# A three-layer transformer block on one core: weight splits of the first stage on VectorE, the norm sum in two products, products of constants at stage ends, and a sparse stage in another order

## The reference

```python
for i in range(DEPTH):                       # layer a, then layer b
    hn = rms_norm(x, norm_gain[i])
    y = mixer_a(hn, ...) if i % 2 == 0 else mixer_b(hn, ...)
    x = x + y
h = rms_norm_2(x, norm_g) * (1.0 + scale) + shift
p = h @ w_in                                 # r, k, v, decay, q, latent, index, gates
y_a = rwkv7_branch(...)
# sparse: index scores, the 128 best keys of each query, softmax over those
score = einsum('bqh,bqhs->bqs', wi_b, relu(einsum('bqhd,bsd->bqhs', qi_b, ki)))
_, sel = lax.top_k(score, topk)
p = softmax(logits + bias); y_b = einsum('bqhk,bqkc->bqhc', p, lat_sel) @ w_uv
x = x + gate * ((sigmoid(g_a) * br_a + sigmoid(g_b) * br_b) @ w_o)
```

## Time and profile before

| | |
|---|---|
| median of 3 runs | 1619.67 us (1618.01 to 1620.99) |
| the profiled execution | 1620.39 us, its span 1618.6 us |
| busy: PE, PEld, DVE, ACT, POOL | 94%, 75%, 50%, 48%, 48% of the span |
| mean granted TensorE clock | 0.981 of full |
| stage_in | 0 to 25.6 us |
| layer a | 26.5 to 661.4 us |
| layer b | 662.4 to 980.2 us |
| modulated projections, sparse attention | 981.2 to 1186.6 us |
| recurrent branch and the rest | from 1187.4 us |

### The profile page before, as it was taken

How to read it: one execution, slowest core, us unless ns; L and a number is a source line. 1 busy time by engine, 2 the same in 40 slices (tenths; PEclk the granted TensorE clock), 3 DMA queues, 4 the chain that set the end, 5 groups by cost and what they waited for, 6 DMA issues and landing times. The chain is left out here.

```text
span 1618.6 us, 29747 instructions
## 1 busy us (share of the span) xinstructions
PE 1520.7 (94%) x11588; PEld 1218.7 (75%) x11588; DVE 804.2 (50%) x1936; ACT 772.5 (48%) x1557; POOL 782.5 (48%) x477
## 2 busy tenths in 40 slices
PE   5999999999999999899999998998968998899997
PEld 4888787878888788667777775676757886678876
DVE  4145455454545456344454323398247753354545
ACT  4654637364553643366665633346654432442322
POOL 4734436262534543466545443236657651475551
PEclk8999999999999999899999999999979999999999
DMA  6333132231413221454444115232010001333331
GB/s 140 110 88 108 53 95 85 76 108 53 121 40 108 64 84 53 89 161 145 137 139 123 53 53 157 52 73 59 8 29 3 4 17 28 79 105 97 97 93 53
DMA packets 239124, 130.98 MB, mean 81 GB/s; under 512 B 28646, under 2 KB 233518, under 8 KB 238968
## 3 DMA queue, kind: packets, MB, share of 16 engines
q1 hardware_dynamic: 231448, 114.09, 25.5%
q10 hardware_dynamic: 7536, 14.98, 3.2%
HBM read 126.62 MB, written 2.43 MB: 80 GB/s over the span
## 5 line engine op out<-in xcount | busy, mean ns | idle before, releaser
L1596 POOL TENSOR_TENSOR w_low<-a_w_raw,w_high 128x1024 fp32r<-128x1024 f32 x70 | 173.2, 2476 | 56.3 <-ACT w_high L1483 56.3
L314 PE MATMUL a_proj<-h_low,w_high 128*128 128x512 f32 x488 | 195.9, 402 | 1.2 <-POOL h_low L1614 1.2
L316 PE MATMUL a_proj<-h_high,w_high 128*128 128x512 f32 x488 | 192.1, 394 | 0.0
L315 PE MATMUL a_proj<-h_high,w_low 128*128 128x512 f32 x488 | 191.3, 392 | 0.0
L1609 POOL TENSOR_TENSOR a_sq_low<-a_sq,a_sq_high 128x512 fp32r<-128x512 f32 x48 | 62.9, 1310 | 249.8 <-ACT a_sq_high L1507 249.8
L895 POOL TENSOR_TENSOR w_low<-b_w_raw,w_high 128x1024 fp32r<-128x1024 f32 x40 | 100.4, 2511 | 97.2 <-ACT w_high L729 97.2
L314 PE MATMUL b_proj<-h_low,w_high 128*128 128x512 f32 x288 | 116.4, 404 | 1.4 <-POOL h_low L934 0.8
L316 PE MATMUL b_proj<-h_high,w_high 128*128 128x512 f32 x288 | 113.1, 393 | 0.0
L315 PE MATMUL b_proj<-h_high,w_low 128*128 128x512 f32 x288 | 113.1, 393 | 0.0
L314 PEld LDWEIGHTS a_proj<-h_low,w_high 128*128 128x128 f32 x488 | 91.7, 188 | 24.0 <-issue 1.4
L316 PEld LDWEIGHTS a_proj<-h_high,w_high 128*128 128x128 f32 x488 | 91.7, 188 | 20.3
(11 more groups left out here) (534 smaller groups left out, 4148.1 us busy)
## 6 DMA issues: line engine op xcount, KB each, us to landing
a_w_raw<-in_a_w_in_dram SPq DMA_DIRECT2D x78, 512.0 KB, 3.8
b_w_raw<-in_b_w_in_dram SPq DMA_DIRECT2D x30, 512.0 KB, 4.1
b_ada_w<-in_ada_w_dram ACTq DMA_DIRECT2D x24, 512.0 KB, 3.7
f_wt<-in_w_in_dram SPq DMA_DIRECT2D x19, 512.0 KB, 3.8
sparse_w_raw<-in_w_in_dram SPq DMA_DIRECT2D x17, 512.0 KB, 3.9
a_bias<-scr_a SPq DMA_DIRECT2D x32, 128.0 KB
a_w_raw<-in_a_w_out_dram SPq DMA_DIRECT2D x8, 512.0 KB, 4.3
b_w_raw<-in_b_w_out_dram SPq DMA_DIRECT2D x8, 512.0 KB, 4.2
```

The costliest lines, as they stand in the source:

```text
L314: nc.tensor.matmul(out, lh, rl, start=first, stop=False)
L315: nc.tensor.matmul(out, ll, rh, start=False, stop=False)
L316: return nc.tensor.matmul(out, lh, rh, start=False, stop=last)
L1596: nc.gpsimd.tensor_tensor(low(slot_of(b)), raw[:, n % RAW, :, :], high(slot_of(b)), ALU.subtract).then_inc(s_wl, 1)
```

## The change

Four groups of edits:

1. stage_in: ACT rounds block 0 only, after its last table copy; DVE rounds block 1 and makes both `w_low`; POOL makes none.
2. Norm sum of layers a and b: the eighth square is no longer added by DVE. TensorE multiplies the sum of seven by ones, then the eighth square by ones, into the same bank.
3. `idle_products`: products of a constant 128 x 128 tile with itself, whose result nobody reads: 24 after the last table copy of bank 0 in stage_in, 20 after each norm sum, 10 ahead of the first product of `first_two` (layers a, b and the modulated projections).
4. sparse_attention: the projection work is spread over one more slot (34, so part 1 of the last step has work too); ACT copies both turned tiles before the exponentials; the tanh moves to step 0; the rounds of the search go from four a step in steps 0 to 7 to four in steps 0 to 3 and two or three in steps 4 to 10; POOL mixes unit 4 before it splits; the last unit's parts are added by DVE.

```diff
 stage_in
-                for j in range(PRE):
-                    pool.wait_ge(s_wh, j + 1)
-                    nc.gpsimd.tensor_tensor(T.wl[:, j, :, :], raw[:, j, :, :], T.wh[:, j, :, :], ALU.subtract).then_inc(s_wl, 1)
...
+                pe.wait_ge(s_ones_r, 1)
+                pe.wait_ge(s_rows, 4)
+                idle_products(nc, T, ps_rows[:, 0, 0:P], 24)
...
+                dve.wait_ge(s_w[1], 16)
+                nc.vector.tensor_copy(T.wh[:, 1, :, :], raw[:, 1, :, :]).then_inc(s_wh[1], 1)
+                for j in (1, 0):
+                    dve.wait_ge(s_wh[j], 1)
+                    nc.vector.tensor_tensor(T.wl[:, j, :, :], raw[:, j, :, :], T.wh[:, j, :, :], ALU.subtract).then_inc(s_wl, 1)
...
+def idle_products(nc, T, out, count):
+    for _ in range(count):
+        nc.tensor.matmul(out, T.pair_ones_r, T.pair_ones_r, start=True, stop=True)
...
 def first_two
+    idle_products(nc, T, outs[0][:, 0:P], 10)
...
 layers a and b, TensorE and VectorE
-            pe.wait_ge(s_acc, KT - 1)
-            nc.tensor.matmul(ps_ss[:, :], T.ones, T.rn[:, :], start=True, stop=True).then_inc(s_nss, 1)
+            pe.wait_ge(s_acc, KT - 2)
+            nc.tensor.matmul(ps_ss[:, :], T.ones, T.rn[:, :], start=True, stop=False)
+            pe.wait_ge(s_nsq, KT)
+            nc.tensor.matmul(ps_ss[:, :], T.ones, sq[:, (KT - 1) % 2, :], start=False, stop=True).then_inc(s_nss, 1)
+            idle_products(nc, T, ps_proj[:, 0, :][:, 0:P], 20)
...
-                if m >= 2:
+                if 2 <= m < KT - 1:
                     add_square(nc, dve, T, sq, s_nsq, s_acc, m - 1)
-            add_square(nc, dve, T, sq, s_nsq, s_acc, KT - 1)
+                if m == KT - 2:
+                    add_square(nc, dve, T, sq, s_nsq, s_acc, m)
...
 sparse_attention
-        rest, slots = NU * KT - sum(issue), 2 * STEPS + 1
+        rest, slots = NU * KT - sum(issue), 2 * STEPS + 2
...
-                for h in range(2):
-                    if t:
-                        keep_pt(t - 1, h)
-                    if t < STEPS:
-                        exps(t, h)
+                if t:
+                    keep_pt(t - 1, 0)
+                    keep_pt(t - 1, 1)
                 if t < STEPS:
                     for h in range(2):
+                        exps(t, h)
+                    for h in range(2):
                         divide(t, h)
...
+            search = {t: (2, 2) for t in range(HP)}
+            search.update({t: (1, 2 if t % 5 == 4 else 1) for t in range(HP, 3 * HP - 1)})
...
-                if t < 2 * HP:
-                    top_rounds(2)
+                early, late = search.get(t, (0, 0))
+                top_rounds(early)
...
+            u = NU - 1
+            dve.wait_ge(s_pt_k, u + 1)
+            nc.vector.tensor_tensor(T.tile(plan[u][1]), now[:, (u - 4) % 2, :], before[:, (u - 4) % 2, :], ALU.add)
```

More of the change, by code:

```diff
@@ L174, in stage_in @@
         s_w = [sem(f"si_w{j}") for j in range(PRE)]
-        s_wh, s_wl = sem("si_w_high"), sem("si_w_low")
+        s_wh, s_wl = [sem(f"si_w_high{j}") for j in range(PRE)], sem("si_w_low")
         A, B, C, TREL = range(4)
@@ L275, in _ @@
                     nc.scalar.activation(sq[:, k, :], T.X0[:, k, :], ACT.Square).then_inc(s_sq, 1)
-                nc.scalar.activation(T.pair_ones_r, T.pair_ones, ACT.Copy)
+                nc.scalar.activation(T.pair_ones_r, T.pair_ones, ACT.Copy).then_inc(s_ones_r, 1)
                 act.wait_ge(s_rowmm, 1)
@@ L322, in first_block, with first_two @@
     return w_in[:, :, L.w_cols(j, 0):L.w_cols(j, 0) + P]
-def first_two(pe, matmul, outs, high, low, T, s_hh, s_low, done):
+def first_two(pe, nc, outs, high, low, T, s_hh, s_low, done):
+    matmul = nc.tensor.matmul
+    idle_products(nc, T, outs[0][:, 0:P], 10)
     for k in range(KT):
@@ L660, in _ @@
             slots = [slot_of(("ring", u)) for u in range(2)]
-            first_two(pe, nc.tensor.matmul, [proj_bank(u) for u in range(2)], [wh[:, i] for i in slots], [wl[:, i] for i in slots],
+            first_two(pe, nc, [proj_bank(u) for u in range(2)], [wh[:, i] for i in slots], [wl[:, i] for i in slots],
                       T, s_hh, s_low, s_proj)
@@ L1472, in _ @@
             pe.wait_ge(s_ln, NQK * PAIRS)
-            pe.wait_ge(s_acc, KT - 1)
-            nc.tensor.matmul(ps_ss[:, :], T.ones, T.rn[:, :], start=True, stop=True).then_inc(s_nss, 1)
+            pe.wait_ge(s_acc, KT - 2)
+            nc.tensor.matmul(ps_ss[:, :], T.ones, T.rn[:, :], start=True, stop=False)
+            pe.wait_ge(s_nsq, KT)
+            nc.tensor.matmul(ps_ss[:, :], T.ones, sq[:, (KT - 1) % 2, :], start=False, stop=True).then_inc(s_nss, 1)
+            idle_products(nc, T, out_bank(3)[:, 0:P], 20)
         @block.scalar
@@ L1940, in _ @@
         def _(pe):
-            first_two(pe, nc.tensor.matmul, [ps[:, u, :] for u in range(2)], [wh[:, slot(u)] for u in range(2)],
+            first_two(pe, nc, [ps[:, u, :] for u in range(2)], [wh[:, slot(u)] for u in range(2)],
                       [wl[:, slot(u)] for u in range(2)], T, s_hh, s_low, s_proj)
@@ L2216, in _ @@
                     turn(t - 1, 1)
-                if t < STEPS:
-                    steps(part_at(t, 1))
+                steps(part_at(t, 1))
                 if t:
@@ L2315, in after @@
                 for u in done_at[pos]:
-                    if u + RING < NU:
+                    if u != 4 and u + RING < NU:
                         split_low(u + RING)
```

41 lines of the change are left out of this document (21 added, 20 removed).

## The result

| | before | changed |
|---|---|---|
| median | 1621.22 us (20 runs, 1618.01 to 1628.03) | 1612.86 us (20 runs, 1608.92 to 1621.13) |
| ratio, 95% interval | | 0.9948 (0.9939 to 0.9958) |
| the profiled execution, its span | 1620.39 us, 1618.6 us | 1611.21 us, 1609.4 us |
| mean granted clock | 0.981 | 0.987 |

The change makes the kernel 8.4 us faster by the medians and 9.2 us by the two profiled executions. Forecast were 12.9 us, 1607.5 us. The sign held, and so did the range for 8 in 10 (1602 to 1616); the forecast's own range (1604 to 1611) was missed by 1.9 us. The gain is a third less than forecast, and its parts have other sizes than the prediction gave them.

The account below looks back on a forecast made before the run. TensorE was taken as the bound nearly everywhere, with gains only at its waits, lower-clock stretches and stage ends on other engines. 3.2 + 5.5 + 0.9 + 3.3 = 12.9 us gave 1607.5 us; own range 1604 to 1611, 8 in 10 1602 to 1616.

Parts of the forecast that it names:

- Term 1: In stage_in, moved roundings and subtractions let ACT, DVE, TensorE and SP all end at 22.4 us, not 25.58: 3.2 us.
- The price of a narrow product: A 128-column fp32r product on TensorE was taken to cost 0.11 us, the spacing of 256 columns.
- Term 2: Idle products keep TensorE's clock up at the starts of layers a, b and the modulated projections: 5.5 us together.
- I take it that it stays at 1.00: With TensorE's gaps cut to about one us or less, the granted clock does not fall at the three starts.
- the clock falls anyway: Rival: term 2 is gone and ten narrow products cost 0.65 us at each start; 1615.0 us, chance 0.18.
- nothing else holds the gain back: Behind the three starts TensorE is the bound, so term 2's 5.5 us are kept.
- The cap by POOL's third block: POOL's slow third-block subtraction limits the higher clock's gain: 2.55 us in a, 2.1 in b, 0.9 at modulated projections.
- Term 3: At the ends of layers a and b, dropping DVE's last addition gains 0.8 and 0.1 us: 0.9 together.
- Term 4: In the sparse stage, earlier copies and spread search rounds cut TensorE's waits, so the stage ends at 1183.3: 3.3 us.
- The estimate of the waits that stay: In the sparse stage 2.9 of 7.3 us stay: about 0.5, 1.2, 0.6 and 0.6 in steps 7, 8, 11, 14.
- Of the other 4.4, 0.6 goes because DVE is as full as before up to step 4: Sparse stage: from 4.4 us of removed waits 0.6 is lost; the last V product moves from about 1185.8 to 1182.0.
- The stage's end: After the sparse stage's V products, ACT copies for 1.4 us and DVE adds in 0.7, ending the stage at 1183.3.

Follow-up runs that it names:

- experiment 3: The changed kernel with 20 narrow idle products instead of 24 in the first stage and 12 instead of 20 behind each norm sum: 1609.35 us.
- experiment 1: The changed kernel without any idle products: 1610.88 us.
- experiment 2: The changed kernel run and profiled once more, unchanged: 1610.80 us.
- experiment 11: The kernel before the change, profiled once more, unchanged: 1618.24 us (one run).
- experiment 7: The kernel before with two sparse-stage edits, ACT's copies ahead of the exponentials and the spread search rounds: 1616.0 us (10 runs).
- the search alone: The kernel before with only the search rounds spread (four in steps 0 to 3, two or three in steps 4 to 10): 1619.82 us (one run).
- the order alone: The kernel before with only ACT copying both turned tiles before the exponentials: 1624.94 us (one run).
- experiment 8: The changed kernel with ACT's wait for layer b's small loads moved behind the first square: 1611.6 us.
- experiment 5: The same run as the order alone, against the kernel before: 1624.94 us (one run).

## Why the prediction was right in sign and too large

**Term 1, the first stage: 3.2 forecast, 2.9 measured.** Right in its mechanism. DVE's subtractions took 1.22 us and not 1.3, ACT and DVE ended at 22.2, TensorE's 24 products 0.5 us later. Over all profiles the first product comes at 28.2 us (five with the old first stage, 27.99 to 29.01) and 25.5 us (nine with the new, 24.78 to 26.46): 2.75 us. Counted from TensorE's last sum of squares to DVE's first `Y`, so without the scatter of what comes ahead, it is 7.95 to 8.06 us with the old stage, 5.10 to 5.12 with 24 narrow products, and 4.86 or 4.87 with 20 (experiment 3) or none (1): the 24 cost 0.25 us. The price of a narrow product was right, 0.11 us. The figure of the Trainium skill ("TensorE: Matmul & The Clock Gate", Back-to-back issue gap), about 81 ns for a product of 128 columns in a stream of weight loads and products, is not what fp32r shows here; the section names no number format, "bf16" is the prediction's word.

**Term 2, the clock: 5.5 forecast; 4.3 at the starts of the first profile (1.1, 2.2 and 1.0), 1.0 of it given back.** Two steps failed. The first is "I take it that it stays at 1.00": it does so in four of nine starts, and in layer a of the first profile it fell without a gap above 0.89 us. The kernel without the products has the same time as with them (1610.88 against 1610.80 us), so the idle products as a whole, with what they cost behind the norm sums, won nothing that could be measured. The rival "the clock falls anyway" held in five starts of nine, and its price for ten narrow products at the lower clock was right: 0.65 us forecast, 0.68 in experiment 2. The measured 8.4 us lie nearer to its 5.4 than to 12.9. The second step is "nothing else holds the gain back": in layer b a small load's wait on ACT held back 1.0 to 1.4 us, shown by moving it. The cap by POOL's third block was right at b (670.07 to 670.18) and, where the clock held, at a (11.10 to 11.12 us, 11.25 forecast).

**Term 3, the norm sum: 0.9 forecast (0.8 and 0.1), 0.7 and 0.0 measured.** The size is right, but the reading of what it is needs a second profile. In experiment 11 the old layer end took 6.05 us and not 6.74, because there the norm product itself had the full clock:

```profile
657.53 1.10 PE L1474 MATMUL a_ss<-rn,consts 128*128 128x512 f32 x2 [2.60 <-DVE rn L308]
```

The two products by themselves shorten an end from 6.05 or 6.15 to 5.27 or 5.37, 0.8 us each; the 20 narrow products behind them, which end later than ACT, take that back.

**Term 4, the sparse stage: 3.3 forecast, 5.1 to 5.4 measured.** The mechanism was right, the size was not. The estimate of the waits that stay was 2.9 us in steps 7, 8, 11 and 14, by `take` in front of the copies; it was 1.4 us, in steps 8 and 11 (1.02 and 0.34 against 1.2 and 0.6), and those of 7 and 14 did not come. But that alone is not the mistake: in experiment 7 2.8 us stayed, nearly what was forecast, and the stage was 5.0 us shorter. What failed is the step from waits to time, "Of the other 4.4, 0.6 goes because DVE is as full as before up to step 4". In the whole change 5.9 us of waits are gone and the last V product comes 5.3 us earlier in the stage (154.2 us after its start, 159.5 before), which looks like these 0.6; experiment 7 has 4.5 us gone for 5.0, the search alone 2.4 for 2.9, the order alone 4.7 for 1.8. The spread of the search wins more than the waits of `s_o` show; through what, no run here isolates. The stage's end was rightly taken as no gain of its own.

**The sum.** The terms in the first profile: 2.9 + 3.3 + 0.8 (with 0.1 of layer a's rest) + 5.1 = 12.1, close to the 12.9 forecast, but by errors of both signs: 2.2 too much at the clock, 1.8 too little in the sparse stage. That nearness is luck. The rest of the way down to 9.2 is the tail's 2.9 us. Chance between two executions can make nearly all of that, since the old tails alone lie up to 2.7 us apart; whether some of it is lasting is not settled. Of the 8.4 us between the medians of 20 runs the two parts that every profile shows, the first stage (2.75 to 2.9) and the sparse stage (5.1 to 5.4), make 7.9 to 8.3, and experiment 1 says that the idle products add nothing measurable.

**Not settled:** what decides, in a given execution, whether the narrow products hold the clock at a start. In experiment 8 the same products with the same gap ahead of layer a (0.89 us) held it, in the first profile they did not. Width was tried, and their number behind the sums, but not their number ahead of a start. Nor is it known why the tails of the kernels with wide products are shorter.

## What to carry to other kernels

When filler work is to keep TensorE's clock up, make its products wide (512 columns here, not 128), size it so that it ends before the engine that sets the barrier, and try the kernel without it: one profile of the changed kernel shows two good starts and the next one. When a stage's start becomes faster, look at what comes at its own time and not with the stage's first work, above all small loads waited for ahead of larger work in an in-order list; move such a wait behind the first work that doesn't need it. Two edits that relieve the same wait should be tried apart and together: here the one that removed the most waiting gave the smaller gain.

## What the runs showed of the hardware

- Products of 128 columns back to back cost 0.11 us each in fp32r, products of 512 columns 0.23 us (six in place of eight behind the norm sum: 1.95 against 2.41 us), so the narrow ones pass half as many columns in the same time. At the lower clock ten narrow products took 2.37 us where they took 1.30 at the higher. With nearly the same time filled (2.99 against 2.87 us in the first stage, 2.41 against 2.74 behind the sums, 1.40 against 1.30 ahead of a start), the wide ones held the clock in nine of nine starts, the narrow ones in four of nine.
- One stretch at the lower clock stands in all fourteen profiles: 13.7 to 20.5 us at the start of the recurrent branch. Others come and go between executions of the same program, also far from any edit. In experiment 5 layer b, whose instructions are those of before, took 303.48 us from its third block to its last residual and not 297.9:

```profile
690.00:698.00 8.00, 7.79 (x29) 5.70 (x30) 1.19 (x4) 1.24 (x3) 8.00 (x8) 0.57 0.64 211
710.00:718.00 8.00, 5.84 (x17) 4.80 (x18) 3.04 (x10) 4.65 (x11) 3.69 (x2) 0.57 0.38 108
```

  Without such dips, a stage's length repeats within some 0.3 us (the sparse stage: 155.75 to 156.07 in nine profiles), which is why the parts could be told apart by lengths and not by times.
- The subtraction of 128 x 1024 elements takes DVE 1.22 us and POOL 4.76 us for two or 5.39 for one while DVE works beside it.
